# Hybrid decoder trunk: feed-forward splits moved ahead, its last block turned inside a down block, norms scaled first, four adaLN sums moved

## What is computed

```python
mod = silu(c) @ w_ada[l] + b_ada[l]        # six pieces: sh1, sc1, g1, sh2, sc2, g2
h = rmsnorm(x, norm1_g[l]) * (1.0 + sc1) + sh1
z = h @ w_in[l]                            # u, v (gated mixer); q, k, v (differential attention)
...
x = x + g1 * (concat([out_a, out_b]) @ w_out[l])
h = rmsnorm(x, norm2_g[l]) * (1.0 + sc2) + sh2
f = swiglu(h, ...) if l == 0 else moe_swiglu(h, ...)   # dense; top 2 of 8 experts
x = x + g2 * f
```

## Time and profile before

| | |
|---|---|
| median of 3 runs | 1323.38 us (1322.63 to 1323.66) |
| the profiled execution, device time | 1322.71 us |
| its span, first to last instruction | 1321.0 us |
| TensorE, VectorE, ScalarE busy | 94%, 82%, 62% |
| mean granted TensorE clock | 0.984 |
| DMA mean | 310 GB/s, 409.61 MB |

### The profile page before, as it was taken

One profiled execution on the slowest core, in us unless ns is written; L12 is line 12 of the kernel. 1 busy time (PEld: TensorE's weight loads), 2 busy tenths in 40 slices (PEclk: granted clock), 3 DMA queues, 4 the chain that ended last, 5 costly groups with the idle time before them and its releaser, 6 DMA issues.

```text
span 1321.0 us, 17449 instructions
## 1 busy us (share of the span) xinstructions
PE 1245.9 (94%) x5431; PEld 872.8 (66%) x5431; DVE 1084.0 (82%) x1385; ACT 817.7 (62%) x1169; POOL 56.6 (4%) x75
## 2 busy tenths in 40 slices
PE   5999969999989888999999999999999999999996
PEld 1444757777767666777676676666676676776664
DVE  2868777888779766788988988988998988988896
ACT  3124534444444553777777777777777777777774
POOL 2102000000000021000000000000000000000000
PEclk8999989999999988999999999999999999999999
DMA  9996739888857525699999999999999999999991
GB/s 294 387 386 209 261 124 317 288 279 298 316 204 262 160 96 203 225 358 365 370 361 366 363 367 367 361 366 367 362 366 368 347 366 368 362 370 367 374 368 63
DMA packets 277871, 409.61 MB, mean 310 GB/s; under 512 B 6676, under 2 KB 209436, under 8 KB 277572
## 3 DMA queue, kind: packets, MB, share of 16 engines
q1 hardware_dynamic: 273732, 393.82, 87.1%
q0 software_dynamic: 4096, 15.25, 3.6%
HBM read 401.70 MB, written 7.34 MB: 310 GB/s over the span
## 4 chain that ended last, share of the span: by engine, by line
PE 75%; DVE 10%; SPq 7%; issue 3%; ACT 3%; DMA 2%; DVEq 0%; POOL 0%; ACTq 0%; POOLq 0%
PE bank L1807 21%; PE bank L1808 21%; PE bank L1809 21%; SPq L607 5%; PE bank L1957 5%; DVE w_lo L1202 3%; DVE ada_acc L1254 1%; ACT w_hi L782 1%; DMA raw<-in_w_ada 1%; DVE more_lo L1202 1%; SPq L591 1%; PE bank L1835 1%; DMA raw<-in_moe_w_up 1%; PE bank L2262 1%; DVE z L1522 1%
## 5 line engine op out<-in xcount | busy, mean ns | idle before, releaser
L1202 DVE TENSOR_TENSOR w_lo<-raw,w_hi 128x1024 fp32r<-128x1024 f32 x366 | 444.8, 1221 | 85.4 <-ACT w_hi L782 82.7
L782 ACT ACTIVATE w_hi<-raw 128x1024 fp32r<-128x1024 f32 x366 | 381.5, 1051 | 99.2 <-PE bank L1809 92.8
L1202 DVE TENSOR_TENSOR more_lo<-raw,more_hi 128x1024 fp32r<-128x1024 f32 x264 | 308.3, 1218 | 2.6 <-ACT more_hi L782 2.5
L782 ACT ACTIVATE more_hi<-raw 128x1024 fp32r<-128x1024 f32 x264 | 260.1, 1047 | 0.1
L1807 PE MATMUL bank<-w_hi,hT_hi 128*128 128x512 f32 x320 | 137.7, 430 | 17.3 <-DVE hT_lo L1289 9.9
L1807 PE MATMUL bank<-more_hi,hgT_hi 128*96 128x512 f32 x368 | 149.8, 407 | 2.0 <-DVE more_lo L1202 2.0
L1808 PE MATMUL bank<-more_hi,hgT_lo 128*96 128x512 f32 x368 | 144.9, 394 | 0.0
L1809 PE MATMUL bank<-more_lo,hgT_hi 128*96 128x512 f32 x368 | 144.8, 394 | 0.0
L1254 DVE SCALAR_TENSOR_TENSOR ada_acc<-raw,silu_c,ada_acc 128x512 f32<-128x512 f32 x152 | 113.9, 750 | 23.3 <-DMA raw<-in_w_ada 16.3
L1807 PE MATMUL bank<-w_hi,hgT_hi 128*96 128x512 f32 x336 | 132.7, 395 | 0.0
L1808 PE MATMUL bank<-w_hi,hgT_lo 128*96 128x512 f32 x336 | 132.6, 395 | 0.0
(11 more groups left out here) (280 smaller groups left out, 1707.8 us busy)
## 6 DMA issues: line engine op xcount, KB each, us to landing
raw<-in_moe_w_gate SPq DMA_DIRECT2D x88, 1024.0 KB, 11.3
raw<-in_moe_w_up SPq DMA_DIRECT2D x88, 1024.0 KB, 13.6
raw<-in_moe_w_down SPq DMA_DIRECT2D x88, 1024.0 KB, 11.9
raw<-in_w_ada SPq DMA_DIRECT2D x48, 1024.0 KB, 10.7
raw<-in_w_in SPq DMA_DIRECT2D x20, 1024.0 KB, 11.7
raw<-in_ffn_w_gate SPq DMA_DIRECT2D x11, 1024.0 KB, 5.4
raw<-in_ffn_w_up SPq DMA_DIRECT2D x11, 1024.0 KB, 8.0
raw<-in_ffn_w_down SPq DMA_DIRECT2D x11, 1024.0 KB, 11.1
```

Source lines behind the costliest of these rows:

```text
L782: act.activation(like(hi_of(s)), src, ACT.Copy).then_inc(hi_done, 1)
L1202: dve.tensor_tensor(like(lo_of(s)), src, like(hi_of(s).bitcast(F32)), ALU.subtract).then_inc(split_done, 1)
```

## The change

- **adaLN blocks.** Layer 0's scale blocks (0,8), (0,9) are taken earlier, (0,7) later. In layer 1's projection each block begins one chunk later and only one of three sums is left in it, at piece 7; the other two take the place of fillers at the router. In the feed-forward (1,4), (1,5) come last, and their two sums stand after it, in place of the 16 fillers, one of them in bank 6.
- **Norms.** `row_scaled` multiplies x by the scale row without the root; `row_norm` then does one multiply by the inverse root and add. Squares go to a scratch tile `junk`. The orders on the three engines are rewritten at three norms: a third weight piece of the first row tile stands ahead of the second tile, whose two halves are transposed together.
- **Feed-forward.** Pieces (1,0) and (1,1) are split right behind block 0's (`AHEAD`, `BEHIND` in `taken` keep the counts). The last hidden tile is transposed between the two down pieces of the block before, and goes to buffers `fT_hi_end`, `fT_lo_end`, made after the last down pieces are split.

The diff, cut to its core. ScalarE's lists follow VectorE's, and the second layer's first norm is rewritten as the one shown, with (2, ...), (3, ...), SC1 and SH1:

```diff
 IN_ORDER = [2, 3, 4, 1, 0]
 Q_AT, K_AT, V_AT, G_AT, U_AT = range(5)
-BESIDE_IN = [[(0, 4), (0, 5), (0, 6), (0, 7), (0, 8)], [(1, 9), (1, 10), (1, 11), None, None]]
-BESIDE_OUT = [(0, 9), None]
-BESIDE_FFN = [(0, 10), (0, 11), (1, 0), (1, 1), (1, 2), (1, 3), (1, 4), (1, 5), (1, 6), (1, 7), (1, 8), None]
+BESIDE_IN = [[(0, 4), (0, 8), (0, 9), (0, 5), (0, 6)], [(1, 9), (1, 10), (1, 11), None, None]]
+BESIDE_OUT = [(0, 7), None]
+BESIDE_FFN = [(0, 10), (0, 11), (1, 0), (1, 1), (1, 2), (1, 3), (1, 6), (1, 7), (1, 8), (1, 4), (1, 5), None]
+SUM_AFTER_FFN = [(1, 4), (1, 5)]
 FIRST_ADA = [2, 0, 3, 1]
...
             for half in range(2):
                 s.append(("in", layer, j, half))
-                if BESIDE_IN[layer][t]:
-                    s.append(("ada", *BESIDE_IN[layer][t], half))
+                m = 2 * t + half - layer
+                if m >= 0 and BESIDE_IN[layer][m // 2]:
+                    s.append(("ada", *BESIDE_IN[layer][m // 2], m % 2))
...
+        AHEAD = WHERE[("gate", 0, 1, 0)]
+        BEHIND = WHERE[("ada", *BESIDE_FFN[0], 1)]
+
         def taken(n, q):
+            if n == AHEAD and q < 2:
+                return 2 * SPLIT_NO[n] - 2 + q + 1
+            if n == BEHIND:
+                return 2 * SPLIT_NO[n] + 2 + q + 1
...
+                            if b == NBLK:
+                                hidden_hi()
+                        if b == 0:
+                            gu_hi(1, 0)
+                            then(act.activation(scratch[:, :], eps_col[:, :], ACT.Silu))
+                            gu_hi(1, 1)
...
-            def row_norm(i, n, a, half, a_piece, b_piece, dst):
+            def row_scaled(i, n, a, half, piece, dst):
+
+                cols = slice(CB * half, CB * half + CB)
+                wait_rows(dve, (x_step, x_own), i - 1, a, half)
+                dve.tensor_tensor(dst[:, a, cols], x[:, a, cols], mod[:, piece, cols], ALU.mult).then_inc(h_scaled, 1)
+
+            def row_norm(i, n, a, half, piece, dst):
                 if half == 0:
                     dve.wait_ge(std_done, NT * i + a + 1)
                     then(dve.reciprocal(rstd[:, a:a + 1], std[:, a:a + 1]))
                 cols = slice(CB * half, CB * half + CB)
-                dve.scalar_tensor_tensor(out=dst[:, a, cols], in0=x[:, a, cols], scalar=rstd[:, a:a + 1],
-                                         in1=mod[:, a_piece, cols], op0=ALU.mult, op1=ALU.mult).then_inc(h_scaled, 1)
                 dve.wait_ge(h_scaled, 4 * i + n + 1)
-                dve.tensor_tensor(dst[:, a, cols], dst[:, a, cols], mod[:, b_piece, cols], ALU.add)\
+                dve.scalar_tensor_tensor(out=dst[:, a, cols], in0=dst[:, a, cols], scalar=rstd[:, a:a + 1],
+                                         in1=mod[:, piece, cols], op0=ALU.mult, op1=ALU.add)\
                    .then_inc((h_done, h_own)[a], 1)
...
+                    if layer and piece > 2:
                         in_lo(layer, piece)
                     beside(3 * layer, piece)
-                    if BESIDE_IN[layer][t]:
-                        ada_half(half, (2 * q, 2 * q + 1))
+                    m = piece // 2 - layer
+                    if layer and piece < 4:
+                        if piece == 3:
+                            ada_half(0, range(4))
+                    elif BESIDE_IN[layer][m // 2]:
+                        ada_half(m % 2, (2 * q, 2 * q + 1))
...
                 if layer == 0:
                     gu_lo(0, 0)
                     out_update(BY_TILE, 0)
+                    out_update(BY_TILE, 1)
                     modulation_out()
-                    out_update(BY_TILE, 1)
+                    dve.wait_ge(ada_out, ada_no[0])
+                    row_scaled(1, 0, 0, 0, SC2, h_tok)
+                    row_scaled(1, 1, 0, 1, SC2, h_tok)
+                    row_norm(1, 0, 0, 0, SH2, h_tok)
                     out_update(BY_TILE, 2)
-                    dve.wait_ge(ada_out, ada_no[0])
-                    row_norm(1, 0, 0, 0, SC2, SH2, h_tok)
-                    out_update(BY_TILE, 3)
                     tile_lo(2, 0, 0)
                     gu_lo(0, 1)
-                    row_norm(1, 1, 0, 1, SC2, SH2, h_tok)
-                    row_norm(1, 2, 1, 0, SC2, SH2, h_tok)
+                    row_norm(1, 1, 0, 1, SH2, h_tok)
+                    out_update(BY_TILE, 3)
                     tile_lo(2, 0, 1)
+                    gu_lo(0, 2)
+                    row_scaled(1, 2, 1, 0, SC2, h_tok)
+                    row_scaled(1, 3, 1, 1, SC2, h_tok)
+                    row_norm(1, 2, 1, 0, SH2, h_tok)
+                    row_norm(1, 3, 1, 1, SH2, h_tok)
                     tile_lo(2, 1, 0)
-                    row_norm(1, 3, 1, 1, SC2, SH2, h_tok)
+                    tile_lo(2, 1, 1)
...
-                                if b or q > 1:
+                                if 4 * b + q == 3 or 4 * b + q > 5:
                                     gu_lo(b, q)
-                                beside(2, 4 * b + q)
...
+                            if b == NBLK:
+                                hidden_lo()
+                        if b == 0:
+                            gu_lo(1, 0)
+                            gu_lo(1, 1)
...
                 if layer:
-                    keep_warm(WARM_NORM, 6)
-                    pe.wait_ge(ada_out, ada_no[0])
+                    ada_sum()
                     tile_turned(3, 0, 0)
+                    ada_sum()
...
                             h_transposes(0, 0, 1)
-                    elif piece == 2:
-                        tile_turned(3, 1, 1)
-                        pe.wait_ge(tr_lo, 4 * 3 + 4)
                     if piece == 3:
...
                     tile_turned(2, 0, 1)
+                    pe.wait_ge(tr_lo, 4 * 2 + 2)
+                    gu_piece(0, 2, 0)
                     tile_turned(2, 1, 0)
+                    tile_turned(2, 1, 1)
                     pe.wait_ge(tr_lo, 4 * 2 + 3)
                     gu_piece(0, 0, 1).then_inc(split_used, 1)
                     gu_piece(0, 1, 1).then_inc(split_used, 1)
-                    tile_turned(2, 1, 1)
                     pe.wait_ge(tr_lo, 4 * 2 + 4)
+                    gu_piece(0, 2, 1).then_inc(split_used, 1)
+
+                    def hidden_turned(b):
+
+                        for a in range(NT):
+                            pe.wait_ge(act_done, NT * b + a + 1)
+                            for c in range(2):
+                                last = pe.transpose(bank[6][:, FB * a + P * c:FB * a + P * c + P],
+                                                    f_act[:, a, P * c:P * c + P], ident[:, :])
+                        last.then_inc(fT_mm, 1)
...
+                            if q == 3 and b and BESIDE_FFN[b - 1] and BESIDE_FFN[b - 1] not in SUM_AFTER_FFN:
                                 ada_sum()
-                            if b < NBLK and (b or q > 1):
-                                if q == 0:
-                                    pe.wait_ge(act_done, NT * b)
+                            if b < NBLK and (b or q > 2):
                                 for a in range(NT):
+                                    if q == 0:
+                                        pe.wait_ge(act_done, NT * (b - 1) + a + 1)
                                     last = gu_piece(b, q, a)
                                     if q == 3 and a == 0:
                                         last.then_inc(gu_mm, 1)
                                 last.then_inc(split_used, 1)
-                            if q == 1 and b:
-                                for a in range(NT):
-                                    pe.wait_ge(act_done, NT * (b - 1) + a + 1)
-                                    for c in range(2):
-                                        last = pe.transpose(bank[6][:, FB * a + P * c:FB * a + P * c + P],
-                                                            f_act[:, a, P * c:P * c + P], ident[:, :])
-                                last.then_inc(fT_mm, 1)
+                            if q == 1 and 0 < b < NBLK:
...
+                                    if b == NBLK - 1 and c == 0:
+                                        hidden_turned(b)
...
-            keep_warm(WARM_HEAD, 6)
+            ada_sum()
...
-            keep_warm(WARM_ROUTER, 6)
+            ada_sum()
...
                 last.then_inc(ga_mm, 1)
+            pe.wait_ge(ada_out, len(ADA))
```

159 lines of the change are left out of this document (98 added, 61 removed).

## The result

The changed kernel took 1312.5 us (median of 4 runs, 1309.9 to 1314.0) against 1323.5 for the kernel before beside it: ratio 0.9907, 95% interval 0.9891 to 0.9923, 11 us less. The prediction was 1308.5, range 1303 to 1317.5. The profiled execution took 1313.2, its span is 9.5 us shorter than that of the earlier trace rows.

What follows compares the result with a forecast made beforehand. Expert stage held by its loads, so every us saved ahead of 537 us counts: 5.6 (seam 1) + 8.5 (seam 2 and layer 2) + 0.7 (router) = 14.8 off profiled 1322.7, 0.7 back to median; forecast 1308.5, range 1303 to 1317.5.

Steps and rivals of the forecast that it cites:

- Seam 1: Norm into feed-forward, three edits together: 5.6 us gained, range 3.5 to 7.
- (c): Block 1's first two splits made before block 0's product: pause 5.38 falls to about 1.5, 1.9 of clock back, gain 5.8.
- (a): First norm: scale row multiplied before the root, scale blocks summed earlier; tile 1.5 us earlier, 0.7 gained because of fillers.
- (b): Third weight piece ahead of the second tile's transposes: pauses 2.4, 0.8, 1.4; gives back (a), 0.2 gained together.
- The last block: Feed-forward's last down block: transposed and split earlier, pause 1.0 for 2.12, then full speed, 2.1 of clock back.
- Scores of layer 2, 8.4 earlier: Layer 2's scores start at 423.4 instead of 431.87, after a 3.8 pause set by VectorE's 30.7 us of work.
- I take 1.3: Layer 2, behind the pause ahead of the scores: one stretch at 1.2 GHz, up to 1.9 lost, booked as 1.3.
- By my list the maxima still come 1 us ahead: Layer 2, pieces 12 and 13: head maxima behind four adaLN steps still precede TensorE; if not, 0.8 to 1.6 lost.
- the 0.95 of the sum: Layer 2, behind the first scores: the adaLN sum after piece 12 is gone, forecast to save 0.86.
- Router, 0.7: Norm at the router: second tile 1.4 earlier, less a chance of half speed; 0.7 taken, bounds -1.5 and 1.5.
- rival (2): With 28 fillers gone, every pause left is followed by 1.2 GHz: 8.9 more, 1317.5; chance 0.07.
- (1): VectorE takes back more, ScalarE's or VectorE's queue delaying the new orders: gain 9.0, 1314.4; chance 0.22.
- (3) to (5): Second split not early, 1314.2, chance 0.05; clock stays slow through projection, slower, 0.03; expert loads no earlier, no change, 0.02.

Runs made afterwards that it cites:

- g_kt: The changed kernel with VectorE's copy of kT in layer 1 made right behind the split of piece 10; ratio 0.9884 to the kernel before.
- n_old: The changed kernel with the norms' multiplication by the modulation row put back behind the root; ratio 0.9950 to the kernel before.
- s_fill: The changed kernel with the sixteen fillers put back ahead of layer 2's first adaLN sum; ratio 0.9938 to the kernel before.
- all7: The changed kernel with seven reorderings together, among them earlier kT, V and G copies and the third piece's split swapped; 1292.0 us, ratio 0.9752 to the kernel before.

## Why the prediction was right, step by step

- **What bounds.** Every us ahead of the experts reached the end (9.25 of lead at 527.5, 9.5 at the end). The reason that I gave, loads that hold the expert stage, isn't what the changed kernel's trace shows: TensorE waits for chunks only at the start, and in the experts only for VectorE (9.7 us of it in the 14 waits of the second line), while SyncE waits for splits to free a chunk (16 waits, 29.5 us, behind the experts' own splits). TensorE is busy 761 of the 773 us from 527 to 1300, so its own work and not a load sets the length of this stage. The forecast needs only that the stage doesn't change, and that holds. TensorE's waits, whole trace:

```profile
PE bank L1889 <- DMA raw<-in_w_ada: 12.8, 5, 5.9
PE bank L1875 <- DVE mT_lo L1794: 9.7, 14, 1.2
```

- **Seam 1, 5.6.** Measured 4.96. (c) was 5.8 by the sum, 6.0 alone, and 5.9 here: a pause of 1.20 for 5.38, and 5.70 for 7.44 behind it. (a) and (b) together, booked at a gain of 0.2, cost 1.0: block 0's last matmul ends 3.07 later, of which 2.11 came in from layer 0. The pauses laid out in block 0 (2.4, 0.8, 1.4) came as 2.64, none and 0.78, but half speed stood behind the 2.64 (up to 1.7), to which I had given 50%. In (a) the edit and the moved modulation brought the 1.5 that I had laid (1.66), and ScalarE's copy took 1.27 of it away again; the fillers hid nothing.
- **The last block.** 3.1 earlier, as forecast to a tenth.
- **Scores of layer 2, 8.4 earlier than behind seam 1.** Measured 8.45 (11.30 - 2.85), with the pause 3.28 for 3.8. But the reason I gave, VectorE's 30.7 us of work, was only half of it: the copy of kT could stand 4.3 us earlier in the same list (g_kt). I had read the order rightly and taken it for a limit.
- **What failed: the terms behind the scores.** "I take 1.3" for one stretch of half speed was 3.1: it lasted from 421 to 428, over the 24 short score matmuls as well. "By my list the maxima still come 1 us ahead" looked at the wrong consumer: the exponentials were in time, the V copy behind the maxima wasn't (1.76 of wait, 1.6 more than the gap before). The 0.5 for small waits never came. Against these stands the 0.95 of the sum. 3.1 + 1.6 - 0.95 = 3.75 of the 3.86 given back.
- **What failed: layer 0 at nothing.** I named the new wait at piece 14 and costed it by ScalarE's copies. The line runs in both layers, and in layer 0 the last sum ahead of it is a scale block, which VectorE modulates behind a head maximum: 0.75. The 1.65 of clock behind the next pause came with it in this execution, and by the runs not because of it.
- **Router, 0.7.** Measured 1.61 to the second tile, just above its upper bound of 1.5; the pre-scaling gave 0.73 of it (n_old).
- **The clock.** The sum counted 1.9 and 2.1 back from the earlier trace rows and 1.7 lost (1.3, and the 0.4 by which 5.8 + 0.2 was lowered to 5.6; rival (2) speaks of 2.5 in the sum, which these terms don't give): 2.3 gained. Measured it is 0.4 lost (13.2 against 12.8, one execution of each): each stretch that went was replaced by one elsewhere. That is 2.7 of the 5.3 that the profiled execution lacks, and the weakest part of the sum. That 0.6 less at seam 1 and 0.75 less in layer 0 stand against 0.9 more at the router and 0.7 more at the start and the end is luck. The measured time lies in the range, 4 us above the forecast, because the range was laid wide enough for rivals 1 and 3, not because these terms were right.
- **Rivals.** (1), ScalarE's or VectorE's queue takes back more: the right mechanism at piece 12 and at the first norm (1.27 behind ScalarE's copy), not at seam 2. (2), the clock: neither refuted nor in the form I gave it. Fillers taken away cost nothing (s_fill); pauses of 2.1 to 3.3 us cost up to 1.5 to 3.4 each, but not always: half speed follows the 2.63 at seam 1 in 8 of 9 traces and the 2.63 at seam 2 in 3 of 9. The Trainium skill's page TensorE: Matmul & The Clock Gate (section Why this matters for your kernels) allows idle gaps up to some 3 us between bursts; here half speed follows 2.12 and 2.57, and in all7 pauses of 0.30 and 1.41 (162.62, 164.68), so the measurement decides, and that figure is no guide here. (3) to (5) fell: the splits came early, nothing stayed slow through a projection, no load held the experts.

## What to carry to other kernels

When a seam is tightened, list for every engine who waits behind each instruction of a moved queue, in each layer in which the line runs: here the waits at piece 14 and piece 12 and ScalarE's copy at the first norm were consumers that I hadn't listed, not durations. Book time at half speed with the pauses that remain, not with the pause that is removed: what one stretch gives back another takes, until pauses themselves become few (all7: 4.2 us against 13). And where an engine with idle time ahead of a wait holds up another, try its order before calling its work the limit: seven reorderings of a few lines each brought 20.5 us (up to 9 of it clock), where the whole change brought 12.3 by the same measure.
